# One decoder layer on one core: the middle four down groups by seven products for token tiles 0 and 1

## The reference

```python
D_MODEL, SEQ, D_FF, FFN_CONV = 1024, 1024, 2816, 3
# ... mixing part: x = x + merged @ w_out
up = rmsnorm(x, g_ffn) @ w_up                       # 1024 -> 2 x 2816
upc, ffn_buf_new = causal_conv(ffn_buf, up, ffn_conv_w)
u, gt = jnp.split(upc, 2, axis=-1)
x = x + (jax.nn.silu(gt) * u) @ w_down              # 2816 -> 1024, contracted over 22 chunks of 128
# then the final rmsnorm of x
```

## Time and profile before

| | before |
|---|---|
| median of 3 runs | 1052.48 us |
| profiled execution | 1052.05 us |
| its span, first to last instruction | 1050.2 us |
| TensorE busy | 1030.4 us (98%), 7402 matmuls |
| VectorE busy | 787.0 us (75%) |
| ScalarE busy | 545.0 us (52%) |
| mean granted TensorE clock | 0.998 |
| mean DMA rate | 112 GB/s |

### The profile page before, as it was taken

One profiled execution on the slowest core, in us unless ns is written; L12 is line 12 of the kernel. 1 busy time (PEld: TensorE's weight loads), 2 busy tenths in 40 slices (PEclk: granted clock), 3 DMA queues, 4 the chain that ended last, 5 costly groups with the idle time before them and its releaser, 6 DMA issues.

```text
span 1050.2 us, 19476 instructions
## 1 busy us (share of the span) xinstructions
PE 1030.4 (98%) x7402; PEld 1000.3 (95%) x7402; DVE 787.0 (75%) x1400; ACT 545.0 (52%) x1047; POOL 65.4 (6%) x162
## 2 busy tenths in 40 slices
PE   7999999999999999999999999999999999999997
PEld 7999988888999999999999999999999999999996
DVE  6754568897678889887787787687787796448974
ACT  7454335555545466555555555555556645125743
POOL 0100000000000001010010010010110000000023
PEclk9999999999999999999999999999999999999999
DMA  7211200120742312132132122122346975514364
GB/s 267 99 41 46 100 21 23 40 82 24 258 144 89 134 41 75 68 142 72 72 136 87 42 92 111 42 101 81 115 140 198 315 231 154 160 54 142 94 184 149
DMA packets 63293, 117.21 MB, mean 112 GB/s; under 512 B 5312, under 2 KB 46912, under 8 KB 63168
## 3 DMA queue, kind: packets, MB, share of 16 engines
q1 hardware_dynamic: 59376, 109.99, 31.2%
q10 hardware_dynamic: 3824, 5.96, 1.6%
HBM read 91.03 MB, written 25.95 MB: 111 GB/s over the span
## 4 chain that ended last, share of the span: by engine, by line
PE 92%; DVE 4%; DMA 2%; ACT 1%; issue 1%; DVEq 0%; SPq 0%; ACTq 0%
PE psum L2879 39%; PE psum L2956 10%; PE psum L2626 9%; PE psum L2829 8%; PE psum L2931 6%; PE psum L2908 3%; PE psum L2847 2%; PE psum L2688 2%; PE psum L2689 2%; PE psum L2690 2%; PE psum L2659 2%; PE psum L2725 1%; PE psum L2775 1%; PE psum L2765 1%; PE psum L2713 1%; DMA act_d<-x_sb 1%
## 5 line engine op out<-in xcount | busy, mean ns | idle before, releaser
L2879 PE MATMUL psum<-diff,w_hi 128*128 128x258 f32 x588 | 116.6, 283 | 2.3 <-ACT psum L1301 2.3
L2879 PEld LDWEIGHTS psum<-diff,w_hi 128*128 128x128 f32 x588 | 94.0, 190 | 2.4 <-issue 2.4
L2879 PE MATMUL psum<-h_hi,w_lo 128*128 128x258 f32 x336 | 95.2, 283 | 0.0
L2879 PE MATMUL psum<-h_hi,w_hi 128*128 128x258 f32 x336 | 95.0, 283 | 0.0
L2879 PE MATMUL psum<-diff,w_lo 128*128 128x258 f32 x336 | 94.9, 282 | 0.0
L2879 PE MATMUL psum<-h_lo,w_hi 128*128 128x258 f32 x336 | 94.8, 282 | 0.0
L2879 PE MATMUL psum<-h_hi,act_hi 128*128 128x258 f32 x336 | 94.6, 281 | 0.2 <-issue 0.2
L2879 PE MATMUL psum<-h_hi,act_lo 128*128 128x258 f32 x336 | 94.7, 282 | 0.0
L2879 PE MATMUL psum<-h_lo,act_hi 128*128 128x258 f32 x336 | 94.5, 281 | 0.0
L2879 PEld LDWEIGHTS psum<-h_hi,w_hi 128*128 128x128 f32 x336 | 63.8, 190 | 0.0
L2879 PEld LDWEIGHTS psum<-diff,w_lo 128*128 128x128 f32 x336 | 63.6, 189 | 0.0
(11 more groups left out here) (400 smaller groups left out, 3330.3 us busy)
## 6 DMA issues: line engine op xcount, KB each, us to landing
raw<-in_w SPq DMA_DIRECT2D x76, 512.0 KB, 4.0
zb<-act_d SPq DMA_DIRECT2D x31, 344.0 KB, 4.9
att<-in_w SPq DMA_DIRECT2D x15, 512.0 KB, 4.7
act_d<-x_sb SPq DMA_DIRECT2D x7, 1032.0 KB, 4.9
raw<-in_w SPq DMA_DIRECT2D x18, 384.0 KB, 3.6
act_d<-att SPq DMA_DIRECT2D x10, 516.0 KB, 2.7
x_sb<-in_x SPq DMA_DIRECT2D x8, 516.0 KB, 4.9
x_d<-x_sb ACTq DMA_DIRECT2D x12, 344.0 KB, 2.6
```

The source lines that it names most:

```text
L2879: ins = mm(bank[to, q], a, b, start=(fresh and k == p == 0), stop=(k == HALF - 1 and p == 2), skip_group_check=True)
```

## The change

The middle group is now done as the other two: pairs T4 to T7 for token tile 2, then units S4 to S7 with products of 9 matmuls. All pairs of rounds are in `MIXED`. All three groups put their items in the same homes. `mid_pair` and its reads are gone. Units 4 to 11 follow each other without pairs between them, and the halves of the last group's items are loaded, rounded and split in units 7 and 8. Banks are dealt out anew, the minus copies of round 2 of the up-projection stand earlier in ScalarE's order, and the final sums use bank 2. The number of item halves rises from 48 to 54; `SKIP_U` goes from 47 to 52.

```diff
-MIXED = (0, 1, 2, 3, 7, 8, 9, 10)
+MIXED = tuple(range(NG))
 T_PAIRS = (range(0, 4), range(4, 8), range(8, 12))
-S_UNITS = (range(0, 4), range(8, 12), range(0))
-FIRST_S, LAST_S = S_UNITS[0], S_UNITS[1]
+S_UNITS = (range(0, 4), range(4, 12), range(0))
+FIRST_S, MID_S, LAST_S = range(0, 4), range(4, 8), range(8, 12)
 MID_PAIRS, END_PAIRS = T_PAIRS[1], T_PAIRS[2]
-DOWN_BANK = (1, 2, 7, 3, 6, 4, 0, 5)
-T_BANKS = ((1, 2), (7, 3), (6, 4), (0, 5)) + 4 * ((), ) + ((1, 2), (0, 5), (3, 6), (1, 2))
-MID_BANKS = ((1, 2), (0, 5), (3, 6))
-S_BANKS = ((1, 2, 7), (3, 6, 4))
+DOWN_BANK = (3, 5, 2, 7, 1, 4, 6, 0)
+T_BANKS = ((3, 5), (2, 7), (1, 4), (6, 0)) + ((6, 0), (3, 5), (7, 1), (6, 0)) + ((3, 5), (6, 0), (7, 1), (3, 5))
+S_BANKS = ((3, 5, 2), (7, 1, 4))
...
-MID_X = (("b11", "b21"), ("b12", "b22"), T_X)
-X_ITEMS = x_items(0, T_X) + x_items(0, S_X) + x_items(1, T_X) + x_items(1, MID_X[0] + MID_X[1]) + x_items(2, S_X) + x_items(2, T_X)
+X_ITEMS = x_items(0, T_X + S_X) + x_items(1, T_X + S_X) + x_items(2, S_X + T_X)
 X_N = numbered(X_ITEMS)
 EARLY = 3
 STAGES = 5
-SKIP_U = 47
+SKIP_U = 52
...
-        homes = (T_X + ("b11", "D1", "D3", "D2", "b21", "b22", "D4"), T_X + ("b11", "b21", "", "b12", "b22", "", ""),
-                 T_X + ("b21", "D3", "b11", "b22", "D4", "D1", "D2"))
+        homes = 3 * (T_X + ("b11", "D1", "D3", "D2", "b21", "b22", "D4"), )
...
                 more = {("S", 0): (1, 1), ("S", 1): (1, 1), ("S", 2): (2, 2), ("S", 3): (1, 2), ("T", 4): (2, 2), ("T", 5): (2, 1),
-                        ("T", 6): (2, 2), ("T", 7): (1, 3), ("S", 8): (1, 1), ("S", 9): (1, 1)}.get((kind, u), (0, 0))[c]
+                        ("T", 6): (1, 1), ("T", 7): (1, 1), ("S", 4): (1, 0), ("S", 7): (0, 5), ("S", 8): (4, 1), ("S", 9): (1, 1),
+                        ("S", 10): (1, 0)}.get((kind, u), (0, 0))[c]
...
+                elif name in T_X:
+                    act.wait_ge(down_done, DONE_N["T", T_PAIRS[g - 1][-1], ("c0", "m1")[T_X.index(name)]])
+                else:
+                    act.wait_ge(down_done, DONE_N["S", 4 * g - 1, S_ORDER[S_X.index(name)]])
...
             read_c21(1, 1)
+            put_v1(2, 0)
             tap(1, 1)
+            put_v1(2, 1)
             for n in range(2, NF):
                 more = n < NF - 1
                 tap(n - 1, 0)
-                put_v1(n, 0)
+                if n > 2:
+                    put_v1(n, 0)
                 part(n, "a22")
-                put_v1(n, 1)
+                if n > 2:
+                    put_v1(n, 1)
+                else:
+                    read_v2(n, 0)
...
             t_copy(2)
+            t_hi(3, 1)
             t_copy(3)
             item_hi(10)
             item_hi(11)
-            t_hi(3, 1)
...
+            for u in range(12):
+                g, p = divmod(u, 4)
+                fin = g == 2
+                s_hi(u, "a22")
+                preload(u)
+                if u == 0:
+                    item_his(0, "D4")
+                    t_copy(7)
+                if u == LAST_S[0]:
+                    item_his(2, "b22", "D4")
+                if fin and p:
+                    mid_square(u - 1, "p4")
+                if u == FIRST_S[-1]:
+                    ta, tb, tc, td = MID_PAIRS
+                    item_his(1, "b11")
+                    t_hi(ta, 0)
+                    item_his(1, "D1", "D2")
+                    t_hi(ta, 1)
+                    item_his(1, "b21")
+                    t_hi(tb, 0)
+                    t_hi(tb, 1)
+                    item_his(1, "D3")
+                    t_hi(tc, 0)
+                    t_hi(tc, 1)
+                    item_his(1, "b22")
+                    t_hi(td, 0)
+                    t_hi(td, 1)
+                    item_his(1, "D4")
+                    for part in ("a11", "S1", "S2", "a12", "S3", "S4"):
+                        s_hi(u + 1, part)
+                    nc.scalar.preload_act_table_set(LN_EXP)
...
+                elif u == MID_S[-1]:
+                    s_hi(u + 1, "a11")
+                    item_his(2, "b11")
+                    s_hi(u + 1, "S1")
+                    item_his(2, "D1")
+                    s_hi(u + 1, "S2")
+                    s_hi(u + 1, "a12")
+                    item_his(2, "D2", "b21")
+                    s_hi(u + 1, "S3")
+                    item_his(2, "D3")
+                    s_hi(u + 1, "S4")
...
+                else:
                     for part in ("a11", "S1", "S2", "a12"):
                         s_hi(u + 1, part)
                     if fin:
                         mid_square(u, "p2")
-                    if p in (1, 2):
-                        item = X_N[1 + f, "t2a", 0] - 1 + 2 * (p - 1)
-                        item_hi(item)
-                        item_hi(item + 1)
+                    if g != 1 and p in (1, 2):
+                        item_his((1, 1, 2)[g], T_X[p - 1])
...
+            for u in range(12):
+                g, p = divmod(u, 4)
+                fin = g == 2
+                if u not in (FIRST_S[0], MID_S[0]):
+                    s_read(u - 1, "p4")
+                s_lo(u, "a22")
+                if u == 0:
+                    item_los(0, "D4")
+                if u == LAST_S[0]:
+                    item_los(2, "b22", "D4")
+                if fin and p:
+                    mid_add(u - 1, "p3")
+                if u == FIRST_S[-1]:
+                    ta, tb, tc, td = MID_PAIRS
+                    s_read(u, "p5")
+                    item_los(1, "b11")
+                    t_lo(ta, 0)
+                    s_read(u, "p6")
+                    item_los(1, "D1")
+                    s_read(u, "p2")
+                    item_los(1, "D2")
+                    s_read(u, "p7")
+                    t_lo(ta, 1)
+                    item_los(1, "b21")
+                    s_read(u, "p3")
+                    s_read(u, "p4")
+                    t_lo(tb, 0)
+                    t_lo(tb, 1)
+                    item_los(1, "D3")
+                    t_read(ta, 0)
+                    t_read(ta, 1)
+                    t_lo(tc, 0)
+                    t_lo(tc, 1)
+                    item_los(1, "b22")
+                    t_read(tb, 0)
+                    t_read(tb, 1)
+                    t_lo(td, 0)
+                    t_lo(td, 1)
+                    item_los(1, "D4")
+                    unit_sums(u + 1)
+                    t_read(tc, 0)
+                    t_read(tc, 1)
+                    for part in ("a11", "S1", "S2", "a12"):
+                        s_lo(u + 1, part)
+                    t_read(td, 0)
+                    t_read(td, 1)
+                    s_lo(u + 1, "S3")
+                    s_lo(u + 1, "S4")
...
+                elif u == MID_S[-1]:
+                    unit_sums(u + 1)
+                    s_lo(u + 1, "a11")
+                    s_read(u, "p5")
+                    item_los(2, "b11")
+                    s_lo(u + 1, "S1")
+                    s_read(u, "p6")
+                    item_los(2, "D1")
+                    s_lo(u + 1, "S2")
+                    s_read(u, "p2")
+                    s_lo(u + 1, "a12")
+                    s_read(u, "p7")
+                    item_los(2, "D2", "b21")
+                    s_lo(u + 1, "S3")
+                    s_read(u, "p3")
+                    item_los(2, "D3")
+                    s_lo(u + 1, "S4")
...
+                    if p == 0:
+                        s_read(u, "p5")
+                        unit_sums(u + 1)
+                        s_read(u, "p6")
+                        s_lo(u + 1, "a11")
+                        s_lo(u + 1, "S1")
+                        s_read(u, "p2")
+                        s_lo(u + 1, "S2")
+                        s_read(u, "p7")
+                        s_lo(u + 1, "a12")
...
-                                pe.wait_ge(down_read, BANK_FREE["T", tp, i])
+                                if tp == MID_PAIRS[0]:
+                                    pe.wait_ge(t_copied, 7 + i)
+                                else:
+                                    pe.wait_ge(down_read, BANK_FREE["T", tp, i])
                                 if tp == END_PAIRS[1]:
                                     pe.wait_ge(fin_added, 4 * len(LAST_S) - 2)
-                            elif m in (1, 2, 5, 6):
-                                pe.wait_ge(read_by_act, act_read(NF - 1, {1: ("c11", 0), 2: ("c11", 1), 5: ("c21", 0), 6: ("c21", 1)}[m]))
-                            elif m in (0, 4):
-                                pe.wait_ge(read_by_dve, dve_read(NF - 1, {0: ("c12", 0), 4: ("c12", 1)}[m]))
+                            elif m in (2, 3, 5, 7):
+                                pe.wait_ge(read_by_act, act_read(NF - 1, {2: ("c11", 0), 3: ("c11", 1), 5: ("c21", 0), 7: ("c21", 1)}[m]))
+                            elif m in (4, 6):
+                                pe.wait_ge(read_by_dve, dve_read(NF - 1, {4: ("c12", 0), 6: ("c12", 1)}[m]))
```

(58 more changed lines are left out.)

220 lines of the change are left out of this document (43 added, 177 removed).

## The result

The changed kernel takes 1062.03 us in the median of 4 runs (1059.48 to 1062.78), the kernel before 1052.84 (4 runs) beside it: ratio 1.008, 95% interval 1.0062 to 1.0098. Timed again in a later series it was 1060.58 against 1052.38, ratio 1.0087 (1.0071 to 1.0103). So it is slower by 0.6 to 1.0%, with 36 matmuls less. The forecast was 1058.4 us.

A forecast was written before the change was run, and what follows sets the result against it. The prediction took TensorE, 92% of the chain that ended last, as the bound. Its terms summed as 1052.05 - 5.67 - 2.25 + 0.3 + 2.55 + 6.5 + 2.9 + 2.0 = 1058.4 us, range 1050 to 1063.

The forecast's parts named there:

- Matmuls, -5.67: Middle pairs and units on TensorE: 36 fewer matmuls at 0.1574 us each, -5.67 us.
- Round 2, -2.25: Up-projection round 2: the minus copy moves ahead of ScalarE's taps, so TensorE's stall goes, -2.25 us (0 to -2.25).
- Banks of the first pairs, 0: First pairs: the 1.4 us wait there becomes a longer wait before unit 0, 0 us (0 to -2.0).
- Differences of pairs 4 to 6, 0: Pairs 4 to 6: four short extra VectorE steps per pair stay hidden, 0 us; at most 6.3 without cover.
- Unit 4, +0.3: Unit 4: unit 5's sums stand ahead of the read of p6 that p7 needs, +0.3 us (0 to 3.1).
- unit 7, +1.8 and +0.75: Unit 7: TensorE waits on VectorE's queue, 1.8 us before p7 and 0.75 us before p4.
- Unit 8, +6.5: Unit 8, before p6 and p7: 4.8 us from VectorE's queue plus 1.7 us from late transfers, +6.5 us.
- rival 2: Units 7 to 9: VectorE alone decides, transfers land in time; not slower, 1051.8 us or 1049.8 us; chance 0.13.
- Unit 11, +2.9: Unit 11, before p6: items 52 and 53 share one stage, delaying ScalarE's minus copy, +2.9 us (1.5 to 5.3).
- TensorE's clock, +2.0: After the roughly 6 us wait before p7 of unit 8: 12 to 20 slow matmuls, +2.0 us (0 to 2.7).
- rival 1: Units 7 and 8: stalls come but TensorE's clock holds, no single wait reaching 4.6 us; 1056.4 us, chance 0.22.
- Rival 3: Units 7 and 8: the hand-over is hidden altogether, so the kernel is faster, 1044.1 us; chance 0.13.

The follow-up runs named there:

- run of round 2 alone: The kernel before with only ScalarE's new order in round 2 of the up-projection (both v1 copies ahead of the tap): 1050.88 us, ratio 0.9986.
- the two with the read moved: Changed kernel, reordered, ScalarE's second v2 read ahead of silu: with six splits on GpSimd 1051.89 us; with all splits on VectorE and unit 0 reordered 1049.56 us.
- the last version: Changed kernel with units 7 and 8 reordered, items 52 and 53 in two stages, v2 read ahead of silu, D3's splits later before unit 0: 1049.56 us.
- the repeat: The changed kernel once more, unaltered, timed against the kernel before: 1060.58 us, ratio 1.0087.
- the GpSimd run: Changed kernel with units 7 and 8 reordered, items 52 and 53 in two stages, six item splits on GpSimd instead of VectorE: 1052.01 us, ratio 0.9999.
- The other GpSimd run: Six item splits on GpSimd, units 7 and 8 reordered, plus ScalarE's second v2 read ahead of silu in round 2: 1051.89 us, ratio 0.9993.
- its filler: Changed kernel with 34 matmuls, whose result nobody reads, issued ahead of the wait of p7 in unit 8: 1058.18 us, ratio 1.0061.

## Why the prediction was right, and where its terms were off

The order of events was the forecast's: less work, a stall in units 7 and 8 behind VectorE's queue, one in unit 11 behind the shared stage, a slow clock behind the longest. The sum came to +6.3 us, the medians give +9.2 and +8.2, the profiles +9.7 and +8.2. So the order of events and the sign were right, and the size was short by a quarter to a third. By its steps:

- **Matmuls, -5.67.** Held: 7366 of them, and the ledger closes with this price to 0.2 us.
- **Round 2, -2.25.** Off by half: -1.2. The step "what could be late next" named the copy of round 3. What was late next was the second v2 read of the same round, at 408.69, behind silu, which waits for VectorE. These rows show it, and the run of round 2 alone and the two with the read moved confirm it.

```profile
407.72 1.07 ACT L1345 ACTIVATE x_sb<-x_sb 128x1032 f32<-128x1032 f32 x1 [0.64 <-DVE x_sb L2212]
408.69 0.37 ACT L1286 ACTIVATE att<-psum 128x258 f32<-128x258 f32 x1
```

- **Banks of the first pairs, 0.** Right in its reasoning: no wait ahead of the first pair, and one of 1.65 and 2.25 ahead of unit 0 in its place in the two profiles (2 to 2.6 was said). In the runs that leave this part alone it was 1.05 to 2.26. Round 2 alone starts unit 0 at 831.68; with the banks changed too it starts at 832.22. That the place in VectorE's queue was the cause is shown by the last version, where D3's halves stand behind S2 and the wait is gone, with 1.0 us of waits inside unit 0 for it.
- **Differences of pairs 4 to 6, 0.** Held: no wait between 409.2 and 832.22 in the changed kernel.
- **Unit 4, +0.3; unit 7, +1.8 and +0.75.** Measured 0.28, 1.77 and 0.55. A count of instructions by their rows in one queue was good to 0.2 us.
- **Unit 8, +6.5.** Measured 0.62 + 6.22 = 6.84, and 5.35 in the repeat, where TensorE came late. The split into 4.8 of VectorE and 1.7 of transfers was 4.4 and 1.65 to 2.4: rival 2, with the transfers free, was wrong in its condition, since VectorE did wait for ScalarE (1.95 us at 958.89). Its sum also leaves out the 2.9 of unit 11 and the 2.0 of the clock without a reason.
- **Unit 11, +2.9.** Measured 2.70, and removed with its stage. The step's working held term by term: load 53 was issued at 998.75, ScalarE went on at 1001.86, and its minus copy ended 5.1 us later. The estimate beside it, from the Trainium skill ("DMA: Bandwidth & Descriptors", "Anatomy of one DMA - SWDGE (gpsimd) path"), uses a fit for transfers issued by GpSimd, while these are issued by SyncE; the sum doesn't use it.
- **TensorE's clock, +2.0.** The fall ahead of p7 of unit 8 cost 2.2, and 2.6 in the repeat. A second one of 1.5 us wasn't foreseen, in unit 11 in one profile and in unit 7 in the other. The step, and rival 1 with it, had taken the 4.6 us of idleness at the end of the kernel before as what a fall needs. Waits of 1.8 to 2.8 us had it too, and at the end of the last version the clock fell 2.4 us after the last matmul.
- **Not in the sum at all:** 0.24 us for each gap, beyond its length. Five new gaps make 1.2 us.

Against the first profile, round 2, the second fall and the gaps make some 3.7 us. These three misses all point the same way, and with the small ones they are the difference between +6.3 and +9.7. That the time lies within 1050 to 1063 owes something to the width of that range.

Rival 3 (all hidden, 1044.1) was wrong for this order but not in kind: with other orders the kernel came to 1049.6. Its argument against, that nothing lies between the units, was about where the work stands and not about how much there is. What keeps the last version from 1044 are 5.4 us of waits in nine gaps (with 0.24 each, 7.6 in sum; the three of before have 5.0): 1052.05 - 5.67 + 7.6 - 5.0 = 1049.0. That they are due to VectorE's load, 39 of 40 us from 940 on, wasn't tried by a run.

## What to carry to other kernels

Before work is moved onto an engine that has room on average, write out its queue across the tightest hand-over: the rows of the trace gave each stall of the hand-over within 0.4 us here. If a stall comes out, try the order first: reads that another engine waits for ahead of work that is wanted later. Here order and one staging buffer were worth 11 us (1060.58 to 1049.56), without an instruction less. And price a stall with what follows it, the restart and the clock, beside its length.

## What the runs showed of the hardware

- **The clock falls behind short waits too.** In the GpSimd run it fell behind one of 1.87 us, with TensorE at work again for 0.8 us: 11 matmuls at the 1.2 GHz level. The other GpSimd run has the same behind 1.88 us.

```profile
951.00:952.00 1.00, 0.45 (x3) 0.48 (x4) 1.00 (x2) 0.68 (x2) 0.92 (x1) 1.00 0.89 259
952.00:953.00 1.00, 1.00 (x6) 1.00 (x5) 1.00 (x1) 0.31 (x1) 1.00 (x2) 0.58 0.67 184
953.00:954.00 1.00, 1.00 (x5) 1.00 (x4) 1.00 (x3) 0.47 (x2) 1.00 (x1) 0.50 1.03 368
```

  The same wait doesn't always bring it. Behind the 1.77 us of unit 7 it fell in one profile of six, behind 2.23 to 2.26 us ahead of unit 0 in two of six, behind 2.7 to 2.8 us in unit 11 in three of five. Behind 1.65 us and less, from 360 us on, it fell in none. The Trainium skill ("TensorE: Matmul & The Clock Gate", "Part 1: The HAM clock gate") says that idleness lowers the clock and work restores it. The trace agrees for the 6.2 us wait and its filler; what decides for the short ones, no run here shows.
- **GpSimd and VectorE get in each other's way.** 684 ns became 1.96 and 2.15 us for a split that reads two tensors from SBUF while GpSimd worked on one, while the reads of an accumulator stayed at 504. The Trainium skill ("GPSIMD Engine Reference", "1. Specifications") says that GpSimd shares its SBUF interfaces with VectorE and contends with instructions of two SBUF inputs. The rows agree.
- **A gap costs 0.24 us beyond its length** at 344 columns. Its length is counted from the modelled end of the last matmul, 0.16 us after the next would have started, and the first matmul behind it takes 0.24 to the next one, not 0.16. So several short waits are dearer than one as long as their sum, as long as the clock holds.
